# Order and piece size of the expert-weight loads in a hybrid decoder trunk

## The reference, cut to what matters

```python
def swiglu(h, w_gu, w_down):
    g, u = jnp.split(h @ w_gu, 2, axis=-1)
    return (jax.nn.silu(g) * u) @ w_down

def moe_swiglu(h, w_router, w_gu, w_down):
    logits = h @ w_router
    top_vals, top_idx = lax.top_k(logits, 2)
    top_w = jax.nn.softmax(top_vals, axis=-1)
    combine = jnp.sum(jax.nn.one_hot(top_idx, 8) * top_w[..., None], axis=-2)
    for e in range(8):
        out = out + combine[..., e:e+1] * swiglu(h, w_gu[e], w_down[e])
```

## Time and profile before

| | us |
|---|---|
| median of 3 runs (1509.62 to 1514.82) | 1512.03 |
| the profiled execution | 1514.56 |
| its span | 1512.8 |
| PE busy | 1457.8 (96%) |
| VectorE (DVE) busy | 988.9 (65%) |
| ScalarE (ACT) busy | 744.4 (49%) |
| HBM read | 498.33 MB |

### The profile page before, as it was taken

How to read it: one execution, slowest core, us unless ns; L and a number is a source line. 1 busy time by engine, 2 the same in 40 slices (tenths; PEclk the granted TensorE clock), 3 DMA queues, 4 the chain that set the end, 5 groups by cost and what they waited for, 6 DMA issues and landing times.

```text
span 1512.8 us, 18723 instructions
## 1 busy us (share of the span) xinstructions
PE 1457.8 (96%) x6964; PEld 985.8 (65%) x6964; DVE 988.9 (65%) x1258; ACT 744.4 (49%) x977; POOL 14.3 (1%) x18
## 2 busy tenths in 40 slices
PE   7989999999999999899999999999899998999996
PEld 2836788788789888676666578732578632778431
DVE  2578788888668989776665589711689510889311
ACT  3574544444356876455544477500577400777200
POOL 0000000000000000002000000000000000000000
PEclk9999999999999999999999999999999999999999
DMA  9878698888266326678999999999999999999997
GB/s 360 324 259 292 246 394 302 308 284 301 72 225 177 98 98 251 260 291 329 410 417 419 403 409 377 375 402 417 402 409 419 395 411 409 409 411 415 382 413 294
DMA packets 139163, 501.81 MB, mean 332 GB/s; under 512 B 13635, under 2 KB 16348, under 8 KB 126136
## 3 DMA queue, kind: packets, MB, share of 16 engines
q1 hardware_dynamic: 137784, 496.51, 85.9%
q0 software_dynamic: 1280, 4.01, 0.8%
HBM read 498.33 MB, written 2.29 MB: 331 GB/s over the span
## 4 chain that ended last, share of the span: by engine, by line
PE 83%; DMA 9%; DVE 4%; ACT 2%; issue 1%; SPq 0%; DVEq 0%; ACTq 0%
PE acc L2636 18%; PE acc L2644 18%; PE acc L2637 17%; PE acc L3132 14%; DMA raw<-in_moe_w_down 4%; DMA mod<-in_moe_w_gu 2%; DMA raw<-in_moe_w_gu 2%; DVE w_lo L1553 1%; PE xb L3022 1%; PE acc L2785 1%; DMA raw_more<-in_moe_w_down 1%; PE xb L3063 1%; DMA raw<-in_ada_w 1%; PE xb L2684 1%; PE acc L3256 1%; PE acc L3251 1%
## 5 line engine op out<-in xcount | busy, mean ns | idle before, releaser
L1553 DVE TENSOR_TENSOR w_lo<-raw,w_hi 128x1024 fp32r<-128x1024 f32 x362 | 435.2, 1222 | 111.4 <-ACT w_hi L1012 100.7
L1012 ACT ACTIVATE w_hi<-raw 128x1024 fp32r<-128x1024 f32 x362 | 377.6, 1058 | 221.4 <-PE acc L2644 156.0
L2636 PE MATMUL acc<-w_hi,g_hi 128*128 128x512 f32 x448 | 179.2, 400 | 3.5 <-issue 3.5
L2637 PE MATMUL acc<-w_hi,g_lo 128*128 128x512 f32 x448 | 174.9, 390 | 0.0
L2636 PE MATMUL acc<-w_hi,a_hi 128*128 128x512 f32 x384 | 153.6, 400 | 0.8
L2637 PE MATMUL acc<-w_hi,a_lo 128*128 128x512 f32 x384 | 149.9, 390 | 0.0
L2644 PE MATMUL acc<-w_lo,g_hi 128*128 128x512 f32 x448 | 138.8, 391 | 1.8 <-DVE w_lo L1553 1.7
L3132 PE MATMUL acc<-raw,g_s 128*64 128x512 f32 x544 | 123.3, 596 | 0.0
L2644 PE MATMUL acc<-w_lo,a_hi 128*128 128x512 f32 x384 | 118.4, 390 | 0.0
L2636 PEld LDWEIGHTS acc<-w_hi,g_hi 128*128 128x128 f32 x448 | 84.3, 188 | 35.5 <-issue 16.1
L2644 PEld LDWEIGHTS acc<-w_lo,g_hi 128*128 128x128 f32 x448 | 83.7, 188 | 22.1 <-DVE w_lo L1553 3.9
(11 more groups left out here) (408 smaller groups left out, 2132.8 us busy)
## 6 DMA issues: line engine op xcount, KB each, us to landing
raw<-in_moe_w_gu SPq DMA_DIRECT2D x134, 1024.0 KB, 12.1
raw<-in_moe_w_down SPq DMA_DIRECT2D x66, 1024.0 KB, 14.7
raw<-in_ada_w SPq DMA_DIRECT2D x96, 512.0 KB, 6.4
mod<-in_moe_w_gu SPq DMA_DIRECT2D x43, 1024.0 KB, 12.0
raw<-in_ffn_w_gu SPq DMA_DIRECT2D x56, 512.0 KB, 5.9
mod<-in_moe_w_down SPq DMA_DIRECT2D x22, 1024.0 KB, 14.0
raw_more<-in_moe_w_gu SPq DMA_DIRECT2D x21, 1024.0 KB, 11.8
raw<-in_ssm_w_in SPq DMA_DIRECT2D x40, 512.0 KB, 4.7
```

The costliest lines, as they stand in the source:

```text
L1012: act.activation(w_hi[:, w % SPLIT, :], raw_tile(no), ACT.Copy).then_inc(hi_ready, 1)
L1553: dve.tensor_tensor(w_lo[:, w % SPLIT, :], raw_tile(no), r32(w_hi[:, w % SPLIT, :]), ALU.subtract).then_inc(raw_used, 1)
L2636: pe.matmul(o, l_hi[:, k, rows_], hi[:, col:col + HALF], start=new, stop=False)
L2637: pe.matmul(o, l_lo[:, k, rows_], hi[:, col:col + HALF], start=False, stop=False)
```

## The change

1. *Groups two by two.* w_gu is worked through as groups (0, 2), (1, 3), (4) and (5, 6). Within a two the steps alternate between the groups, so that two steps on end are the same rows and 2048 neighbouring columns: one DMA of 8 KB per descriptor. Group 4, and loads to "row_b" and "rest8", keep 4 KB. The accumulators follow: in a two, each group has a buffer of its own.
2. *Experts in turn in every pair.* Units are now 16, 16, 8, 16 steps of w_gu, then 14 + 14 of w_down for a large expert and 8 + 8 + 6 + 6 for a small one. The order of a pair is: large 16, small 16, small 16, large 16, small 8, large 8, small 16, large 16, small 8, large 14, small 8, large 14, small 6, small 6. `LARGE_AHEAD` is gone.
3. *Places.* Puts, adds, gathers, slots, hidden pieces and read-outs are given new places in the list.
4. *Order known sooner.* `order_of_experts` runs on the vector engine between the first gathered block and the second, and no longer at step 4 of the list. What it held besides (`most_slots`) and the weights of tokens, which stood ahead of `positions`, go to steps 19 and 17. The scalar engine warms up SiLU ahead of its early w_hi tiles and makes two of them between the gathered blocks.

```diff
+    GROUP_TWOS = ((0, 2), (1, 3), (4,), (5, 6))
+    GROUP_OF = [(js[n % len(js)], n // len(js)) for js in GROUP_TWOS for n in range(len(js) * KD)]
+    GROUP_OF += [(FJ, k) for k in range(FK)]
+    GROUP_END = {j: 1 + max(n for n, (of, _) in enumerate(GROUP_OF) if of == j) for j in range(FJ + 1)}
+    GROUP_END[-1] = 0
+    GROUP_HALF = (0, 0, 1, 1, 0, 1, 0)
+    GROUP_USE = (0, 1, 0, 1, 2, 2, 3)
+    GROUPS_DUE = {GROUP_END[js[0]] + 2: js for js in GROUP_TWOS}
+    HIDDEN_AT = (35, 37, 39, 59, 61, 63, 65)
     def units(p):
-        steps = [KD] * FJ + [FK // 4] * 4
+        steps = [2 * KD, 2 * KD, KD, 2 * KD] + ([KD, KD, KD - 2, KD - 2] if p % 2 else [FK // 2, FK // 2])
     def pair_order(r):
         large, small_ = units(2 * r), units(2 * r + 1)
-        ahead = LARGE_AHEAD if r == 0 else len(large)
-        order_ = [tile for u in large[:ahead] for tile in u]
-        for u, later in enumerate(small_):
-            order_ += later + (large[ahead + u] if ahead + u < len(large) else [])
+        order_ = large[0] + small_[0]
+        for u in range(1, len(small_)):
+            order_ += small_[u] + (large[u] if u < len(large) else [])
         return order_
-    SMALL_SLOT_AT = (35, 51, 59, 61)
-    ORDER_AT, SECOND_AT, SLOTS_AT, PLACES_AT, POS_AT = 4, 6, 18, 21, 23
-    PUT_AT = ((27, 45), (6, 10))
-    ADDS_AT = ((74, 76, 78, 80), (14, 18, 22, 26), (13, 23, 29, 41))
+    SMALL_SLOT_AT = (36, 58, 60, 62)
+    GATHERS_AT = {0: (68, 72, 76), 1: (64, 68, 72)}
+    ORDER_AT, SECOND_AT, SLOTS_AT, PLACES_AT, POS_AT = 19, 10, 17, 18, 19
+    PUT_AT = (27, 45)
+    ADDS_AT = ((5, 7, 9, 11), (74, 76, 78, 80))
+    SMALL_ROWS_AT = (15, 13)
...
-            if step_ < FJ * KD and step_ % KD == KD - 1:
-                due.setdefault(m + 3, []).append(("group", p, step_ // KD))
+            if step_ + 1 in GROUP_END.values() and step_ < FJ * KD:
+                j = GROUP_OF[step_][0]
+                at_ = next(at_ for at_, js in GROUPS_DUE.items() if j in js)
+                due.setdefault(m + at_ - step_, []).append(("group", p, j))
...
-                q = (1 if j == FJ else j) % 2
-                return (q + r) % 2, before_pair((q + r) % 2, r) + (3 if j == FJ else j // 2)
+                q = 1 if j == FJ else GROUP_HALF[j]
+                return (q + r) % 2, before_pair((q + r) % 2, r) + (3 if j == FJ else GROUP_USE[j])
...
-                    gi, k = divmod(n, KD)
-                    dst = two_tiles(homes[0])
-                    src = w_gu[k * P:(k + 2) * P, MIX_COLS[gi]:MIX_COLS[gi] + TW].rearrange("(h p) n -> p h n", h=2)
+                    gi, k = GROUP_OF[n]
+                    if GROUP_OF[n + 1][0] == gi:
+                        dst = two_tiles(homes[0])
+                        src = w_gu[k * P:(k + 2) * P, MIX_COLS[gi]:MIX_COLS[gi] + TW].rearrange("(h p) n -> p h n", h=2)
+                    else:
+                        dst = two_tiles(homes[0]).rearrange("p h n -> p (h n)")
+                        src = w_gu[k * P:(k + 1) * P, MIX_COLS[gi]:MIX_COLS[gi] + 2 * TW]
...
-            early_hi("moe", MOE_BEFORE)
-
             warm(ACT.Silu)
-
-            def first_gather(first):
+            early_hi("moe", MOE_BEFORE, 2)
+
+            def first_gather(first, between=0):
                 for n in range(len(G_BLOCKS)):
                     piece(first + n)
                     gathered_hi(first + n, n)
-
-            first_gather(pc0["moe"])
+                    if 2 + n < between:
+                        early_hi("moe", 2 + n, 3 + n)
+
+            first_gather(pc0["moe"], EARLY["moe"])
...
                 if s == ORDER_AT:
-                    order_of_experts()
+                    most_slots()
                 if s == SLOTS_AT:
+                    weights_of_tokens()
                     rows_of_slots(0)
...
             positions()
-            for n in range(len(G_BLOCKS)):
+            gathered_lo(pc0["moe"], 0, highs_moe + 1)
+            early_lo("moe", MOE_BEFORE, 2)
+            order_of_experts()
+            for n in range(1, len(G_BLOCKS)):
                 gathered_lo(pc0["moe"] + n, n, highs_moe + n + 1)
-                if n:
-                    early_lo("moe", n, 2 * n)
+                early_lo("moe", n + 1, n + 2)
```

More of the change, by code:

```diff
@@ L511, in body_pieces @@
             for n in range(len(G_BLOCKS)):
-                after.setdefault(FJ * KD + 8 + 4 * n, []).append(("gather", n))
+                after.setdefault(GATHERS_AT[0][n], []).append(("gather", n))
         else:
@@ L539, in round_pieces @@
                 found += [("h", *which) for _, kind, *which in PIECES[True].get(step_, []) if kind == "h"]
[L540 to L545, removed]
+                found += [("put", p + n_) for n_ in range(2) if step_ == PUT_AT[n_]]
+                if p and step_ in ADDS_AT[0]:
+                    found.append(("add", p - 1, ADDS_AT[0].index(step_)))
+                if step_ == SMALL_ROWS_AT[p > 0]:
+                    found.append(("small",) if p else ("picked",))
             else:
                 found += [("slot", q) for q in range(SMALL_SLOTS) if step_ == SMALL_SLOT_AT[q]]
[L548 to L552, removed]
+                if step_ in ADDS_AT[1]:
+                    found.append(("add", p - 1, ADDS_AT[1].index(step_)))
+                found += [("gather", g) for g in range(len(G_BLOCKS) if p < STORED else 0) if step_ == GATHERS_AT[1][g]]
             for what in found:
@@ L1263, in body @@
                         act.activation(ada_high(ended)[:, :], ada[:, ended % 2, :], ACT.Copy).then_inc(ada_hi_ready, 1)
+                    for gi in GROUPS_DUE.get(s, ()) if B.mixture else ():
+                        mix_gates(B, gi)
                     j, k = divmod(s, KD)
-                    if 1 <= j <= FJ and k == 2:
-                        if B.mixture:
-                            mix_gates(B, j - 1)
-                        else:
-                            act.wait_ge(w_used, B.full(j - 1))
-                        for t in range(0 if B.mixture else T):
+                    if not B.mixture and 1 <= j <= FJ and k == 2:
+                        act.wait_ge(w_used, B.full(j - 1))
+                        for t in range(T):
                             act.activation(h[:, t, :], acc[B.pair(j - 1, t)[0]][:, 0:HALF], ACT.Silu).then_inc(gate_ready, 1)
@@ L1959, in body @@
                         split_lo(B.raw_no(s), B.spl + s, e)
+                    for gi in GROUPS_DUE.get(s, ()) if B.mixture else ():
+                        mix_products(B, gi)
                     j, k = divmod(s, KD)
-                    if 1 <= j <= FJ and k == 2:
-                        if B.mixture:
-                            mix_products(B, j - 1)
-                        for t in range(0 if B.mixture else T):
+                    if not B.mixture and 1 <= j <= FJ and k == 2:
+                        for t in range(T):
                             q, _ = B.pair(j - 1, t)
@@ L2004, in group_products @@
                 else:
-                    dve.wait_ge(nat_used, B.native + KD * (j + 1))
-                gates_in = {1: 0, 3: 2, 5: 4, 6: 4}[j]
-                dve.wait_ge(s_done[0], B.half(gates_in)[1] + 1)
+                    dve.wait_ge(nat_used, B.native + GROUP_END[j])
+                half, used = B.half({1: 0, 3: 2, 5: 4, 6: 4}[j])
+                dve.wait_ge(s_done[half], used + 1)
                 for side, slot in SMALL_UP[j]:
```

57 lines of the change are left out of this document (28 added, 29 removed).

## The result

The changed kernel takes 1518.03 us, median of 10 runs (1515.56 to 1524.3); the kernel before takes 1512.03 (10 runs, 1509.62 to 1514.82). The ratio is 1.0040, 95% interval 1.0028 to 1.0052: slower by 0.4%, where 1498 and faster was forecast.

What follows compares the result with a forecast made beforehand. PE was taken to bound the kernel until about 1023 us, then the loads. Start 642.7 plus pairs of 212, 211, 212.7 and 210.8 gave 1489.2; with 9.5 us following, span 1498.7, median about 1498, range 1481 to 1515.

Steps and rivals of the forecast that it cites:

- 6: How PE and loads meet in pairs 1 to 3: the loads bind, pairs take 211, 212.7 and 210.8 us.
- step 4: PE's own time in pairs 1 to 3: 210.5 us a pair, with the new waits at accumulators.
- (b): Small expert's down product opens the accumulator group 6 just used: PE waits 1.6 us, bounds 0.3 and 2.9.
- (d): Next large expert's group 2 opens the small expert's output accumulator at step 1, before read-out: PE waits 2.0 us.
- Rival C: Small 32 after the large 16 starves PE once a pair: 221 us a pair, time 1526; chance 0.12.
- Step 5: Loads in pairs 1 to 3: 8 KB pieces at 419.7 for 409 GB/s, 2.8 us a pair less.
- rival A: The 8 KB gain is absent, as contiguity made w_down faster: +7.6 us, 1506; chance 0.16.
- Step 3: Pair 0 on PE: 212 us with new waits, against 209.0 before; bounds 207 and 216.
- (a): Pair 0, routing's vector instructions at steps 18 and 19 delay w_lo of steps 19 and 20: together 3.5 us.
- rival D: In-order read-outs cost more, in known places and other changes: PE 216 us a pair, 1516; chance 0.13.
- Step 1: Start, ahead of PE's first large step: fewer early scalar tiles bring it 1.2 us sooner.
- Step 2: Order of experts known sooner: the 5 us are hidden behind waits for homes, counted 0, bound -2.

Runs made afterwards that it cites:

- e2: Changed kernel with the products of the small expert's groups 5 and 6 six places later and the second pick two steps later: 1511.92 us, ratio 0.9994.
- e5: Changed kernel with large and small units in plain turns in pairs 1 to 3, no small unit ahead: 1509.19 us, ratio 0.9970.
- e6: e4 and e5 together, with the late products of pairs 1 to 3 moved thirteen places instead of six: 1499.18 us, ratio 0.9908.
- e9: Changed kernel with 4 KB pieces: a load takes two row blocks of one group, PE meets tiles in twos of a group: 1519.78 us, ratio 1.0050.
- e10: e6 with the edit of e9 (4 KB pieces): 1504.79 us, ratio 0.9942.
- e1: Changed kernel with the routing's vector instructions of steps 18 and 19 of the first large expert moved to step 17: 1514.31 us, ratio 1.0006.
- e4: Changed kernel with the edits of e1, e2 and e3 together: 1504.39 us, ratio 0.9939.
- e3: Changed kernel with the small expert's output read out one step sooner: 1513.85 us, ratio 0.9998.

## Why the prediction was wrong

*The step that failed is 6*, "in pair 1 it touches 0 once: 0.5 us. From then the loads set the pace, and no home-full gap is left but at the 16". What the runs show instead: PE sets the pace to the end, and the touch at 0 comes in every pair and costs 4.7 us each time, not 0.5 once. The arithmetic of the lead was nearly right. From the start of the small 32 to that of the third large unit PE eats 32 + 16 + 8 + 8 + 16 = 80 tiles in 969.2 - 884.9 = 84.3 us; at 1.25 us a tile the loads bring them in 100. So 15.8 us of lead are used up, of a lead estimated at 16.5, and the touch at 0 is there. Two things were mis-judged. First, it happens in every pair: PE is slower than the loads over the pair, so the homes fill again each time, with stops of 3.9 to 5.7 us. Second, a touch at 0 isn't worth the lateness of one tile. It also bares everything that w_hi's and w_lo's buffers had covered, and the slower clock behind it. e2, which only takes the products away from that place, is worth 7.0 us.

In numbers, pairs 1 to 3 took 649.9 us where step 4 has 3 x 210.5 = 631.5 for PE and the forecast 634.5. The difference to 631.5 is 9.1 us of waits in the third large units, 5.0 of slow clock behind them, and 6.9 of PE's own work taken too low (649.9 less 17.3 of waits and 5.0 of clock is 627.6, where 3 x 206.9 = 620.7 was taken), less 2.6 that (b) and (d) cost less than taken. The stops sum to 13.8 us, near the 15.4 over the forecast, but that is the balance of the sum above and no cause: e5 and e6 have stops of 6.1 and 5.6 us in pair 1, which takes 213.8 and 212.7.

*Rival C* named the side and the mechanism's kin, and it had 0.12. Its place was wrong: the lead at the start of the small 32 was full, as inferred, and PE didn't idle in the small unit; and so was its price, 221 a pair against 216.6.

*Step 5* (8 KB) was right, 409 to 419 and 422 GB/s, also with 28 KB between the pieces, so rival A falls. By the Trainium skill's rule ("DMA: Bandwidth & Descriptors", Why small descriptors are slow) it would have been 1.2%; these rows measure 2.6%, and the measurement decides. In time it was worth some 5 us in this order (e9, with (d) counted back) and 5.1 in the other (e10), not the 8.4 of step 5.

*Step 3.* (a) was taken at 3.5: the two waits are 0.60 + 2.67 = 3.3, and a stretch at clock 0.83 comes on top; e1 takes 5.4 us out of pair 0. (b), taken at 1.6, is 1.43. Pair 0 came to 214.0 for 212, inside its bounds of 207 and 216. *Step 4:* (b) 1.42 for 1.6 and (d) 1.29 for 2.0, both a little less than taken. Small pieces were taken at 8 us a pair and are 9.3 in pair 1 (its small units sum to 83.6, of which 0.57 is waiting and 73.7 are the steps). What step 4 left out is the products of the small expert's last two groups ahead of the third large unit's w_lo; it counted (d) and (b) and no other change of expert. That is *rival D*, which had 0.13: its 1516 was the nearest time, its 216 a pair on PE is the measured 216.6 on average, and e1 to e4 show that such read-outs together were worth 15.3 us. Its reason was only in part right: (a), (b) and (d) stayed at or under what was taken for them, and the rest stands where the lead touches 0. Moving the read-outs gives 15.3, changing the order (which moves read-outs too) 10.6, both 20; how much of the 20 is the lead alone isn't separated.

*Step 1* gave 1.2 us; measured from the same point it is 0.56. *Step 2*, 0, was fair: the order is cast at 642.2 and SP issues at 643.41, and no wait of PE went with it.

*Of the signs* of being right that the prediction named, the 419 GB/s came. Three did not: "no slice under 390 GB/s after the first large unit of pair 1" (282 and 292 GB/s over 10 us in pairs 2 and 3), pairs 2 and 3 at 212 to 213 us (216.7 and 215.9), and pair 0 within 3 us of 209 (214.0). The two that were to make the whole wrong (pair 0 over 216, PE without idle from pair 2 on) didn't, so they were badly chosen: neither looks at the homes or at the size of PE's waits.

Left open: where 3 of the 6.4 us of e3 come from (the profiled execution has only 3.5 of them in the experts' part), and what 8 KB pieces alone do in the old order of experts. The latter wasn't tried.

## What to carry to other kernels

A ring of buffers between loads and an engine whose appetite swings (385 and 596 GB/s here) has to be simulated along the whole order, against both its ends; the average rates don't show where it runs empty. Full homes cost nothing by themselves here; the empty end did, once a pair. Long runs of the hungry kind are what makes the swing, so alternate as evenly as the accumulators allow. And where the lead is thin, look at each in-order engine for work queued in front of the next tile: moving it a few places was worth 15 us here for a change of a handful of numbers.

## What the runs showed of the hardware

- PE's granted clock fell during or right behind waits of 2.58 and 2.67 us, and in pair 2 of one of 1.55 (0.50 from 1190 to 1192 us), in otherwise busy stretches (0.54 and 0.60 in the two stretches of 2 us behind the 2.58, the lower level of 1.2 GHz for most of it), and matmuls of 0.23 us started 0.43 us apart. The length of the wait alone doesn't decide: in e2 it stayed at 1.00 after 1.63 us (at 1188.12) and in e9 after 2.59 (at 978.34), but in e4 it fell to 0.72 and 0.50 after a wait of 1.65 us at 969.19. The Trainium skill says the same in kind ("TensorE: Matmul & The Clock Gate", HAM oscillation — how this bites in real kernels): an engine that is made to wait for data between runs of matmuls pays for the wait and again for the slower clock; the trace agrees, with 1.7 us behind the wait of 2.58.
- Loads of w_gu with 28 KB between rows ran at 409 and 410 GB/s in 4 KB pieces (e9, 950 to 970 us) and at 419 and 422 in 8 KB pieces (after, the same stretches). I had left open whether the gain is one of contiguous sources; it isn't.
